# Weight-block sums on VectorE, finer waits of the partial copies and parts of 6, 6, 6 and 4 chunks in a two-layer decoder step

## The chip, the cores and the metric

The kernel runs on one core of a Trainium2 chip. The metric is device microseconds of one execution; three runs of the kernel before were timed, and one execution was profiled.

## What is computed

One step of a two-layer decoder trunk for 576 tokens (512 prompt tokens and 64 sample tokens, both with the same weights), width 1024, all in float32. Each layer is a feed-forward block (FFN), a mixer with three branches, and a second FFN. The change is in the two FFNs of each layer, four in all.

```
def swiglu(x, w_in, w_out):
    gate, up = jnp.split(x @ w_in, 2, axis=-1)          # w_in: 1024 x 5632
    return (jax.nn.silu(gate) * up) @ w_out             # w_out: 2816 x 1024

def hybrid_layer(x, p, ...):
    x = x + 0.5 * swiglu(rms_norm(x, p['ffn1_norm']), p['ffn1_w_in'], p['ffn1_w_out'])
    ...                                                  # mixer: attention, RG-LRU, short convolution
    x = x + 0.5 * swiglu(rms_norm(x, p['ffn2_norm']), p['ffn2_w_in'], p['ffn2_w_out'])
```

## The kernel before

Tokens lie along the free axis, so that a matmul has 128 weight columns and moves 288 tokens (half of 576). Float32 accuracy comes from a split: every operand is a rounded part and a rest (weights `whi` and `wlo`, inputs `hh`/`hl`, `bh`/`bl`, `ah`/`al`), and each product is three matmuls. ScalarE makes `whi` from the loaded weights `wraw`, VectorE makes `wlo` by subtraction.

The 2816 hidden columns of an FFN are taken in 11 steps of 256. The work is a list of units, written out in `ffn_units`:

- **up** s: the plain product for step s, four items (each 24 matmuls);
- **gate** s: the same size, but by a scheme with seven block products instead of eight (items 0 to 6, 12 matmuls each). It needs sums and differences of the four weight blocks (`wsum`, the weights of items 1 to 4), and of the moving blocks;
- **out** v: a part of the hidden steps times `w_out`, for 256 output columns, also by seven products; four units (v = 0 to 3) for each part;
- **last** v: the last part of the hidden steps, plain, without sums.

`PART_STEPS` says which hidden steps make a part: before these are 2, 3, 3 and 3 steps (a step is two chunks of 128, so 4, 6, 6 and 6 chunks), and the last is plain.

All engines walk the same list of items in order, each with its own queue. TensorE works on item i, ScalarE and VectorE split the item that takes i's place in a ring of four weight slots (`BEHIND[i]`, mostly item i+4). A unit's loads go into one of two `wraw` halves by DMAs that the SP queue issues in order.

Between the products of a gate unit ScalarE copies partial sums out of PSUM (`parts`, after items 0, 1, 2 and 4) into `kept`, `tmp5` and `tmp2`; item 2 must not start before the copy after item 0, item 3 not before the copy after item 1. Those buffers hold step s-1's hidden values until VectorE has made their split blocks, in four pieces (`moving_lo`, nth 1 to 4); `buffers_free` makes ScalarE wait for that. Step s-1's hidden values are computed on VectorE by `even_hidden` (behind item 6 of the gate) and `odd_hidden` (behind item 0 of the next up).

The weight sums are made by GpSimd (POOL) in `weight_sums`. `past_forgets` looks up 16 cache pages on SP, and the mixer's VectorE code waits for their DMAs. At the end of the second FFN VectorE also prepares sums of the next layer's inputs (`norm_sums`), and in the prologue it works out `decay` from a parameter.

Of the kernel before, what the change touches and what calls it, by code (L numbers as in the profile page):

```python
# [130 lines left out]
def ffn_items():  # L131
# [3 lines left out]
    for n, (kind, s, v) in enumerate(FFN_UNITS):  # L135
        if kind == "up" and s in (3, 6, 9):
            at += 1
# [60 lines left out]
def build(nc, t_in, t_out):  # L198
    S, plan = make_plan()
    with ExitStack() as ctx:  # L200
# [44 lines left out]
        with ExitStack() as m:  # L245
# [220 lines left out]
        def _(sp):  # L466
# [49 lines left out]
            def past_forgets(L):  # L516

                st, k = S["ffn1"], 2 * len(FFN_UNITS) - 1
# [8 lines left out]
            with sp.Fori(0, DEPTH) as L:  # L527
# [9 lines left out]
                past_forgets(L)  # L537
# [53 lines left out]
        def _(pe):  # L591
# [73 lines left out]
            def ffn(name, nn, L):  # L665
                st, f = S[name], nn // 2
                i = 0
                for n, (kind, s, v) in enumerate(FFN_UNITS):
# [6 lines left out]
                    for j in range(2):  # L675
                        slot = st.slot(2 * n + j)
                        for h in range(2):
# [7 lines left out]
                            for kk in range(half):  # L685
# [3 lines left out]
                                if kind == "last" and v == 0 and j == 0:  # L689
                                    pe.wait_ge(a_ready, L * 12 + (6 * f + c + 1))  # L690
# [281 lines left out]
        def _(act):  # L972
# [65 lines left out]
            def buffers_free(st, f, n, L):  # L1038

                kind, s, v = FFN_UNITS[n]  # L1040
                if kind == "out" and v == 0:
                    act.wait_ge(mov_ready, blocks_ready(L, f, PART_STEPS[s][-1], 4))
                elif kind == "gate" and FFN_UNITS[n - 1][0] == "out":
                    act.wait_ge(freed[st.slot(2 * n - 2)], st.turn(2 * n - 2, L) + 1)
                elif kind == "gate" and 0 < s <= 8:
                    act.wait_ge(mov_ready, blocks_ready(L, f, s - 1, 4))
                elif kind == "gate" and s > 8:
                    act.wait_ge(a_ready, L * 12 + (6 * f + 2 * (s - 8)))

            def parts(st, f, n, m, L):  # L1050
# [8 lines left out]
                if m == 0:  # L1059
                    buffers_free(st, f, n, L)  # L1060
# [3 lines left out]
            def ffn(name, nn, L):  # L1064
# [3 lines left out]
                for n, (kind, s, v) in enumerate(FFN_UNITS):  # L1068
                    for m in range(7 if n in SEVEN_NO else 4):
# [8 lines left out]
                        elif kind == "gate" and m == 6:  # L1078
                            if s < 8:
                                moving_first(f, s, s - PART_STEPS[(s + 1) // 3][0], L)  # L1080
                            act.wait_ge(gate_in, L * 44 + (22 * f + 2 * s + 2))
                            act.activation(tmp[5][:, 0:N], tmp[5][:, 0:N], ACT.Silu).then_inc(silu_ready, 1)
                        elif kind == "up" and m == 0 and 0 < s <= 8:
                            moving_second(f, s - 1, s - 1 - PART_STEPS[s // 3][0], L)
                        elif kind == "last" and m % 2:
# [6 lines left out]
                            else:  # L1092
                                norm_next(L, c, 24, L + 1, 0)
                                if c % 2:
                                    norm_sums(L * 16 + 16, c // 2)
# [220 lines left out]
        def _(dve):  # L1316
# [69 lines left out]

            def ring_split(st, f, i, L):
# [658 lines left out]
```

## Time and profile before

| | |
|---|---|
| median of 3 runs | 3035.36 us (3030.13 to 3038.66) |
| profiled execution | 3030.68 us, its span 3028.6 us |
| TensorE busy, of the span | 93% |
| VectorE busy | 72% |
| ScalarE busy | 44% |
| GpSimd busy | 19% |
| mean granted TensorE clock | 0.977 of full |

Busy shares are means over stages; the four FFNs lie at about 26 to 490, 1050 to 1525, 1525 to 1975 and 2560 to 3005 us of the span, the mixers between them.

### The profile page before, as it was taken

The numbers are of one execution on the slowest core, as the hardware profiler recorded it, in microseconds if no ns is written. First come the engines' busy times: TensorE is split into PE (matmuls) and PEld (weight loads), VectorE is DVE, ScalarE is ACT, GpSimd is POOL, SyncE is SP. The second block draws the span as 40 slices with busy tenths as digits, with TensorE's granted clock in tenths as the row PEclk, the third lists the DMA queues.
The fourth block names the chain that finished last, engine by engine and source line by source line (L and its number), as shares of the span: only waits on it lengthen the run. The fifth ranks groups of instructions, "written<-read, shape, count | busy, mean of one in ns | idle before, by whom it ended". The sixth has DMA issues, their size and how long they took to land.

```text
span 3028.6 us, 59749 instructions
## 1 busy us (share of the span) xinstructions
PE 2827.6 (93%) x20752; PEld 2742.9 (91%) x20752; DVE 2168.4 (72%) x3317; ACT 1331.2 (44%) x2393; POOL 579.7 (19%) x472
## 2 busy tenths in 40 slices
PE   4989999999999998989988989999999999989997
PEld 4888999898999998989988989999889999989897
DVE  5878776766655588778778778767766447878777
ACT  4444444455532344434444444435555223444444
POOL 2323321000000123323123323210000002323231
PEclk8999999999999999999999999999999999999999
DMA  2222222333222222222212222233332223122222
GB/s 87 84 77 77 73 89 79 103 95 88 83 83 83 85 77 78 76 79 84 85 64 77 77 78 84 85 91 87 88 94 80 83 83 98 57 84 85 74 91 77
DMA packets 299402, 250.31 MB, mean 83 GB/s; under 512 B 20899, under 2 KB 296563, under 8 KB 299175
## 3 DMA queue, kind: packets, MB, share of 16 engines
q1 hardware_dynamic: 297031, 242.44, 26.2%
q0 software_dynamic: 2144, 4.98, 0.5%
q8 instruction: 125, 2.05, 0.3%
q14 instruction: 102, 0.84, 0.1%
HBM read 240.04 MB, written 7.34 MB: 82 GB/s over the span
## 4 chain that ended last, share of the span: by engine, by line
PE 60%; DVE 17%; DVEq 8%; issue 7%; ACT 5%; SPq 1%; POOLq 1%; ACTq 0%; DMA 0%
PE ps L608 30%; PE ps L656 16%; PE ps L693 9%; DVE wlo L1394 5%; ACT whi L1021 2%; DVEq L1499 2%; DVE x L1498 2%; DVEq L1503 1%; DVE kept L1417 1%; DVE bl L1404 1%; DVEq L1432 1%; DVEq L1415 1%; DVE kept L1420 1%; PE ps L821 1%; DVE tmp L1445 1%
## 5 line engine op out<-in xcount | busy, mean ns | idle before, releaser
L1394 DVE TENSOR_TENSOR wlo<-wraw,whi 128x512 fp32r<-128x512 f32 (+2 forms) x500 | 382.1, 766 | 224.5 <-ACT whi L1021 218.6
L1325 DVE TENSOR_TENSOR wlo<-wraw,whi 128x1024 fp32r<-128x1024 f32 (+1 forms) x188 | 221.2, 1177 | 317.9 <-ACT whi L985 317.1
L1939 POOL TENSOR_TENSOR wsum<-wraw 128x512 f32<-128x512 f32 (+2 forms) x184 | 229.8, 1249 | 1049.6 <-DVE wlo L1394 683.3
L985 ACT ACTIVATE whi<-wraw 128x1024 fp32r<-128x1024 f32 (+1 forms) x188 | 191.6, 1020 | 393.6 <-PE ps L608 379.3
L608 PE MATMUL ps<-hh,whi 128*128 128x288 f32 x1664 | 362.1, 299 | 0.0
L608 PE MATMUL ps<-hl,whi 128*128 128x288 f32 x1664 | 357.7, 297 | 0.0
L608 PE MATMUL ps<-hh,wlo 128*128 128x288 f32 x1664 | 357.5, 296 | 0.0
L1021 ACT ACTIVATE whi<-wraw 128x512 fp32r<-128x512 f32 (+2 forms) x500 | 283.5, 571 | 119.8 <-PE ps L656 75.2
L1394 DVE TENSOR_TENSOR wlo<-wsum,whi 128x512 fp32r<-128x512 f32 (+2 forms) x368 | 270.5, 746 | 62.1 <-ACT whi L1021 61.3
L693 PE MATMUL ps<-hh,whi 128*128 128x288 f32 x1408 | 304.2, 298 | 8.9 <-DVE hl L1588 4.7
L693 PE MATMUL ps<-hl,whi 128*128 128x288 f32 x1408 | 303.7, 298 | 0.0
L656 PE MATMUL ps<-bh,whi 128*128 128x288 f32 x896 | 271.1, 303 | 34.8 <-DVE wlo L1394 21.5
L693 PE MATMUL ps<-hh,wlo 128*128 128x288 f32 x1408 | 302.8, 297 | 0.0
L656 PE MATMUL ps<-th,whi 128*128 128x288 f32 x704 | 220.3, 313 | 80.1 <-ACT kept L1062 80.1
L608 PEld LDWEIGHTS ps<-hh,whi 128*128 128x128 f32 x1664 | 269.1, 190 | 0.9
L608 PEld LDWEIGHTS ps<-hl,whi 128*128 128x128 f32 x1664 | 269.3, 190 | 0.0
L608 PEld LDWEIGHTS ps<-hh,wlo 128*128 128x128 f32 x1664 | 269.3, 190 | 0.0
L656 PE MATMUL ps<-bh,wlo 128*128 128x288 f32 x896 | 265.2, 296 | 0.0
L656 PE MATMUL ps<-bl,whi 128*128 128x288 f32 x896 | 264.8, 296 | 0.0
L1021 ACT ACTIVATE whi<-wsum 128x512 fp32r<-128x512 f32 (+2 forms) x368 | 198.2, 552 | 137.2 <-PE ps L693 86.3
L693 PEld LDWEIGHTS ps<-hh,whi 128*128 128x128 f32 x1408 | 228.9, 190 | 9.8 <-DVE hl L1588 5.0
L693 PEld LDWEIGHTS ps<-hh,wlo 128*128 128x128 f32 x1408 | 229.0, 190 | 0.0
(363 smaller groups left out, 6757.3 us busy)
## 6 DMA issues: line engine op xcount, KB each, us to landing
wraw<-in_ffn_w_in SPq DMA_DIRECT2D x88, 1024.0 KB
wraw<-in_ffn_w_out SPq DMA_DIRECT2D x48, 768.0 KB
wraw<-in_w_in SPq DMA_DIRECT2D x28, 1024.0 KB
wraw<-in_w_in SPq DMA_DIRECT2D x56, 512.0 KB
wraw<-in_w_branch SPq DMA_DIRECT2D x24, 512.0 KB
wraw<-in_w_out SPq DMA_DIRECT2D x9, 1024.0 KB
wraw<-in_ffn_w_out SPq DMA_DIRECT2D x16, 512.0 KB
kv<-in_cache_k SPq DMA_DIRECT2D x128, 64.0 KB, 1.9
```

Source lines behind the costliest of these rows:

```text
L608: last = pe.matmul(ps[slot][:, half, 0:HF], weights, rhs[:, k, half * HF:(half + 1) * HF], start=(start and c == 0 and n == 0), stop=(stop ...
L656: last = pe.matmul(bank, weights[:, kk, :], moving, start=(m in (0, 1, 5) and kk == 0 and t == 0), stop=(m in (3, 5, 6) and kk == half - 1 ...
L693: last = pe.matmul(ps[slot][:, e, 0:HF], weights[:, kk, :], moving[:, c, e * HF:(e + 1) * HF], start=(c == 0 and t == 0), stop=(c == 2 * h ...
L821: pe.matmul(logits(e, qb), qp[hs, qs], kp[hs, 0:n], start=True, stop=False, skip_group_check=True)
L985: act.activation(split_tile(into, j, rowwise), raw_tile(slot, j, rowwise), ACT.Copy).then_inc(hi_ready, 1)
L1021: ins = act.activation(ring(whi, i), weights_of(st, i), ACT.Copy)
L1325: dve.tensor_tensor(split_tile(lo, j, rowwise), raw_tile(slot, j, rowwise), split_tile(hi, j, rowwise).bitcast(F32), ALU.subtract).then_in ...
L1394: ins = dve.tensor_tensor(ring(wlo, i), weights_of(st, i), ring(whi, i).bitcast(F32), ALU.subtract)
L1404: dve.tensor_tensor(bl[:, a:b, kk, :], raw, bh[:, a:b, kk, :].bitcast(F32), ALU.subtract).then_inc(mov_ready, 1)
L1498: dve.tensor_tensor(down[:, HF:N], down[:, HF:N], other[:, 0:HF], ALU.add)
L1499: dve.drain()
L1939: pool.tensor_tensor(out, x0, x1, op).then_inc(wsum_ready, 1)
```

## The change

Its parts: (1) hidden steps go into parts of 3, 3, 3 and 2 steps, so the out units come after up 3, 6 and 9 and the plain last part has four chunks; (2) the four weight sums of every gate and out unit move from GpSimd to VectorE, each placed behind a ring split, two items ahead; (3) ScalarE waits for piece 1 before the copy after item 0 and for piece 3 before the copy after item 1, where before it waited for piece 4 ahead of the first; VectorE makes pieces 2 and 3 both behind item 1 of the up unit, and piece 4 behind item 2; (4) the page lookups move from behind the mixer's first loads to between the loads of up 10 and gate 10 of the first FFN; (5) `decays` moves from the prologue to behind gate 4 of the first FFN (of both layers); (6) the next layer's `norm_sums` come two or four tiles later.

```diff
-PART_STEPS = ((0, 1), (2, 3, 4), (5, 6, 7), (8, 9, 10))
+PART_STEPS = ((0, 1, 2), (3, 4, 5), (6, 7, 8), (9, 10))
+LAST = 9
+SUMS_BEHIND = {3: (0,), 5: (1,), 7: (2, 3)}
...
-        if s in (2, 5, 8):
-            units += [("out", s // 3, v) for v in range(4)]
+        if s in (3, 6, 9):
+            units += [("out", s // 3 - 1, v) for v in range(4)]
...
                     if kind == "up":
                         load(S[name], n, L, 0, (w1, 0, KD, s * 256 + FFN, 256))
+                        if name == "ffn1" and s == STEPS - 1:
+                            past_forgets(L)
...
-                st, k = S["ffn1"], 2 * len(FFN_UNITS) - 1
+                st, k = S["ffn1"], 2 * FFN_UNITS.index(("out", 2, 3))
                 wait_apart(sp, filled[st.slot(k)], st.turn(k, L) + 1)
...
-            def buffers_free(st, f, n, L):
+            def buffers_free(st, f, n, m, L):
                 kind, s, v = FFN_UNITS[n]
-                if kind == "out" and v == 0:
+                if kind == "out" and v == 0 and m == 0:
                     act.wait_ge(mov_ready, blocks_ready(L, f, PART_STEPS[s][-1], 4))
-                elif kind == "gate" and FFN_UNITS[n - 1][0] == "out":
+                elif kind == "gate" and m == 1 and FFN_UNITS[n - 1][0] == "out":
                     act.wait_ge(freed[st.slot(2 * n - 2)], st.turn(2 * n - 2, L) + 1)
-                elif kind == "gate" and 0 < s <= 8:
-                    act.wait_ge(mov_ready, blocks_ready(L, f, s - 1, 4))
+                elif kind == "gate" and m < 2 and 0 < s <= LAST:
+                    act.wait_ge(mov_ready, blocks_ready(L, f, s - 1, (1, 3)[m]))
...
+            def weight_sum(st, f, i, L, first=None):
+                n, m, _ = ITEMS[i]
+                if n not in SEVEN_NO or m not in SUM_AT:
+                    return
+                base = st.first_unit + n
+                a11, a12, a21, a22 = (block_of(st, n, kh, mh_) for mh_ in range(2) for kh in range(2))
+                x0, x1, op = ((a21, a22, ALU.add), (summed(n, 1), a11, ALU.subtract), (a12, summed(n, 2), ALU.subtract), (a11, a21, ALU.subtract))[m - 1]
+                dve.drain()
+                if first is not None:
+                    wait_done(dve, st, f, first, L)
+                if m == 1:
+                    dve.wait_ge(unit_loaded[base % 2], L * (plan["layer_units"] // 2 * 32) + (base // 2 + 1) * 32)
+                dve.tensor_tensor(summed(n, m), x0, x1, op).then_inc(wsum_ready, 1)
...
                 elif m == 1:
                     moving_lo(f, s - 1, 2, M_T2, M_T3 + 1, two(tmp[2][:, 0:N]), L)
+                    moving_lo(f, s - 1, 3, M_B21, M_B22 + 1, two(tmp[5][:, 0:N]), L)
                 elif m == 2:
-                    moving_lo(f, s - 1, 3, M_B21, M_B22 + 1, two(tmp[5][:, 0:N]), L)
-                else:
                     moving_lo(f, s - 1, 4, M_T4, M_T4 + 1, tmp[3][:, 0:HF].rearrange("p (a n) -> p a n", a=1), L)
...
                         for j in BEHIND[i]:
+                            if j == 4:
+                                weight_sum(st, f, j + 1, L, first=i)
                             ring_split(st, f, j, L)
+                            if j + 2 < len(ITEMS):
+                                weight_sum(st, f, j + 2, L)
...
                             even_hidden(f, s, L)
+                            if f == 0 and s == 4:
+                                dve.drain()
+                                decays()
...
                                 norm_next(L, c, 24, L + 1, 0)
-                                norm_sums(L, L * 16 + 16, c, L + 1, 0)
+                                for kk in SUMS_BEHIND.get(c, ()):
+                                    norm_sums(L, L * 16 + 16, 2 * kk, L + 1, 0)
+                                    norm_sums(L, L * 16 + 16, 2 * kk + 1, L + 1, 0)
...
             with pool.Fori(0, DEPTH) as L:
-                weight_sums(S["ffn1"], 0, L)
```

On VectorE the order changes behind item 6 of a gate unit and item 0 of the next up unit. Before (L1394 is a ring split, L1417 and L1420 are `even_hidden`, L1428 begins `odd_hidden`):

```order
L1394 TENSOR_TENSOR wlo<-wraw,whi 128x512
L1416 ISA
L1417 TENSOR_TENSOR kept<-kept,tmp 128x576
L1420 TENSOR_TENSOR kept<-kept 128x288
L1393 REGISTER_ALU
L1394 TENSOR_TENSOR wlo<-wraw,whi 128x512
L1427 REGISTER_ALU
L1428 TENSOR_TENSOR tmp<-tmp 128x576
```

And now (L1411 is the ring split, L1402 the sum, L1434 and L1437 are `even_hidden`, L1445 begins `odd_hidden`):

```order
L1411 TENSOR_TENSOR wlo<-wraw,whi 128x512
L1401 REGISTER_ALU
L1402 TENSOR_TENSOR wsum<-wraw 128x512
L1433 ISA
L1434 TENSOR_TENSOR kept<-kept,tmp 128x576
L1437 TENSOR_TENSOR kept<-kept 128x288
L1410 REGISTER_ALU
L1411 TENSOR_TENSOR wlo<-wraw,whi 128x512
L1402 TENSOR_TENSOR wsum<-wsum,wraw 128x512
L1444 REGISTER_ALU
L1445 TENSOR_TENSOR tmp<-tmp 128x576
```

One sum stands ahead of `even_hidden` (its register row belongs to the wait for the unit's load), one ahead of `odd_hidden`. Further on, behind items 1 to 3 of the up unit, VectorE had these rows before (L1404 are pieces 2, 3 and 4, L1445 reads the second up tile):

```order
L1394 TENSOR_TENSOR wlo<-wsum,whi 128x512
L1403 REGISTER_ALU
L1404 TENSOR_TENSOR bl<-tmp,bh 128x2x288
L1393 REGISTER_ALU
L1394 TENSOR_TENSOR wlo<-wsum,whi 128x512
L1403 REGISTER_ALU
L1404 TENSOR_TENSOR bl<-tmp,bh 128x2x288
L1445 TENSOR_TENSOR tmp<-tmp,ps 128x576
L1393 REGISTER_ALU
L1394 TENSOR_TENSOR wlo<-wsum,whi 128x512
L1403 REGISTER_ALU
L1404 TENSOR_TENSOR bl<-tmp,bh 128x288
```

Now the same stretch reads (L1421 are the pieces, L1462 the second up tile):

```order
L1411 TENSOR_TENSOR wlo<-wsum,whi 128x512
L1402 TENSOR_TENSOR wsum<-wraw,wsum 128x512
L1420 REGISTER_ALU
L1421 TENSOR_TENSOR bl<-tmp,bh 128x2x288
L1420 REGISTER_ALU
L1421 TENSOR_TENSOR bl<-tmp,bh 128x2x288
L1410 REGISTER_ALU
L1411 TENSOR_TENSOR wlo<-wsum,whi 128x512
L1402 TENSOR_TENSOR wsum<-wraw 128x512
L1420 REGISTER_ALU
L1421 TENSOR_TENSOR bl<-tmp,bh 128x288
L1462 TENSOR_TENSOR tmp<-tmp,ps 128x576
```

All pieces stand ahead of the second up tile, and two sums have come in between. On SP, before, the lookups stand behind the mixer's first two loads (L525 is the first of 16 lookup DMAs):

```order
L503 DMA wraw<-in_w_in 128x8x256
L347 ISA
L523 TENSOR_LOAD pages
L523 ISA x2
L525 ISA
L525 DMA lfp<-in_cache_logf 128x8
```

Now they stand behind the load of up 10, and gate 10's load (the L505 row at the end) behind the last of them:

```order
L505 DMA wraw<-in_ffn_w_in 128x8x256
L349 ISA
L527 TENSOR_LOAD pages
...
L529 DMA lfp<-in_cache_logf 128x8
L499 ISA
L505 ISA
L505 DMA wraw<-in_ffn_w_in 128x8x256
```

The L349 row is the wait for the end of the last out unit; what follows on SP, gate 10's load first, queues behind it and the 16 lookups.

## Rows read from the trace of the kernel before

**Rows 1.** The page: busy us, share of the span, instructions.

```profile
PE 2827.6 (93%) x20752; PEld 2742.9 (91%) x20752; DVE 2168.4 (72%) x3317; ACT 1331.2 (44%) x2393; POOL 579.7 (19%) x472
```

**Rows 2.** The waits of TensorE: total us, times, longest us.

```profile
PE ps L656 <- ACT kept L1062: 80.1, 32, 3.2
PE ps L656 <- DVE wlo L1394: 47.1, 40, 20.5
PE ps L656 <- ACT tmp L1062: 13.2, 13, 1.6
...
PE ps L693 <- DVE al L1411: 8.3, 8, 1.1
...
PE ps L781 <- DVE lf L1649: 7.4, 2, 3.7
...
PE ps L693 <- DVE wlo L1325: 4.2, 1, 4.2
```

**Rows 3.** Timeline of TensorE, then ScalarE, at one gate unit.

```profile
1210.80 0.61 PE L656 MATMUL ps<-th,whi 128*128 128x288 f32 x1 [2.94 <-ACT kept L1062]
...
1210.34 0.41 ACT L1062 ACTIVATE kept<-ps 128x288 f32<-128x288 f32 x1 [4.38 <-DVE bl L1404]
```

**Rows 4.** Timeline of VectorE behind the up unit ahead of it: start, us.

```profile
1200.50 0.69 DVE L1394 TENSOR_TENSOR wlo<-wraw,whi 128x512 fp32r<-128x512 f32 x1 [1.85 <-ACT whi L1021]
1201.11 0.75 DVE L1428 TENSOR_TENSOR tmp<-tmp 128x576 f32<-128x576 f32 x1
1201.93 0.46 DVE L1433 TENSOR_TENSOR tmp<-tmp,kept 128x288 f32<-128x288 f32 x1
1202.31 0.45 DVE L1434 TENSOR_TENSOR tmp<-tmp,kept 128x288 f32<-128x288 f32 x1
...
1203.23 0.75 DVE L1404 TENSOR_TENSOR bl<-kept,bh 128x576 fp32r<-128x576 f32 x1
1203.90 0.75 DVE L1445 TENSOR_TENSOR tmp<-tmp,ps 128x576 f32<-128x576 f32 x1
...
1209.86 0.45 DVE L1404 TENSOR_TENSOR bl<-tmp,bh 128x288 fp32r<-128x288 f32 x1
```

**Rows 5.** Timeline of VectorE, then GpSimd, behind that gate unit.

```profile
1223.38 1.60 DVE L1417 TENSOR_TENSOR kept<-kept,tmp 128x576 f32<-128x576 f32 x1 [0.16 <-issue]
1225.06 1.39 DVE L1420 TENSOR_TENSOR kept<-kept 128x288 f32<-128x288 f32 x1
...
1222.58 1.79 POOL L1939 TENSOR_TENSOR wsum<-wsum,wraw 128x512 f32<-128x512 f32 x1 [0.28 <-issue]
```

**Rows 6.** VectorE by line and shape: count, busy us, mean ns.

```profile
L1417 DVE TENSOR_TENSOR kept<-kept,tmp 128x576 f32<-128x576 f32 x44 | 59.2, 1346 | 7.3 <-issue 6.6 <-ACT tmp L1082 0.7
L1498 DVE TENSOR_TENSOR x<-x,tmp 128x288 f32<-128x288 f32 x48 | 56.9, 1185 | 0.0
```

**Rows 7.** Windows: us, busy PE, PEld, DVE, ACT, POOL, granted clock, DMA.

```profile
900.00:950.00 50.00, 50.00 (x377) 50.00 (x376) 22.53 (x26) 13.82 (x15) 0.00 (x0) 1.00 0.26 83
...
1212.00:1214.00 2.00, 2.00 (x11) 2.00 (x11) 0.69 (x1) 0.11 (x2) 0.00 (x0) 0.58 0.00 0
1220.00:1222.00 2.00, 2.00 (x17) 2.00 (x16) 1.91 (x5) 1.21 (x2) 0.99 (x1) 1.00 0.04 11
```

**Rows 8.** Timeline of TensorE at two out units, one after the other.

```profile
1281.35 0.40 PE L656 MATMUL ps<-bh,whi 128*128 128x288 f32 x1 [0.34 <-DVE wlo L1394]
...
1290.33 0.39 PE L656 MATMUL ps<-bh,whi 128*128 128x288 f32 x1 [0.34 <-DVE wlo L1394]
```

**Rows 9.** Timeline of SP: issue of a gate unit's load.

```profile
1215.73 0.39 SPq L503 DMA_DIRECT2D wraw<-in_ffn_w_in  x1
```

**Rows 10.** Timeline of SP, then VectorE, at the page lookups.

```profile
493.55 18.13 SPq L525 DMA_DIRECT2D lfp<-in_cache_logf  x16
...
512.90 0.23 DVE L1633 COPY lfp<-lfp 128x128 f32<-128x128 f32 x1 [7.14 <-DMA lfp<-in_cache_logf]
```

**Rows 11.** Timeline of VectorE in the prologue: the longest run of the decay's small operations.

```profile
58.66 1.62 DVE L1556 SCALAR_TENSOR_TENSOR spt<-spt 128x8 f32<-128x8 f32 x7
```

More of the change, by code:

```diff
@@ L135, in ffn_items @@
     for n, (kind, s, v) in enumerate(FFN_UNITS):
-        if kind == "up" and s in (3, 6, 9):
+        if kind == "up" and s in (2, 5, 8):
             at += 1
@@ L1421, in even_hidden @@
                 else:
-                    kept_whole(2 * (s - 8), kept[:, 0:2, :])
+                    kept_whole(2 * (s - LAST), kept[:, 0:2, :])
             def odd_hidden(f, s, L):
@@ L1428, in odd_hidden @@
                 dve.tensor_tensor(pf[:, 0:N], pf[:, 0:N], tmp[1][:, 0:N], ALU.mult)
-                if s >= 8:
-                    kept_whole(2 * (s - 8) + 1, two(pf[:, 0:N]))
+                if s >= LAST:
+                    kept_whole(2 * (s - LAST) + 1, two(pf[:, 0:N]))
                     return
@@ L1537, in ffn @@
                                 norm_next(L, c, 24, L + 1, 0)
-                                norm_sums(L, L * 16 + 16, c, L + 1, 0)
+                                for kk in SUMS_BEHIND.get(c, ()):
+                                    norm_sums(L, L * 16 + 16, 2 * kk, L + 1, 0)
+                                    norm_sums(L, L * 16 + 16, 2 * kk + 1, L + 1, 0)
                         i += 1
@@ L1561, in log1p, with decays @@
                 dve.drain()
+            def decays():
+                dve.wait_ge(consts_ready, 2)
+                log1p(spt[1][:], spt[2][:], spt[3][:], spt[4][:], spt[2][:])
+                dve.tensor_scalar(spt[3][:], lam, -1.0, 0.0, ALU.mult, ALU.max)
+                dve.drain()
+                dve.tensor_tensor(spt[4][:], spt[3][:], spt[2][:], ALU.add)
+                dve.drain()
+                dve.tensor_scalar(decay[:, :, 0, :], spt[4][:], -8.0, None, ALU.mult)
+                dve.tensor_scalar(decay[:, :, 1, :], spt[4][:], 8.0, None, ALU.mult)
             dve.memset(eps[:, 0:1], EPS)
@@ L1600, in _ @@
             dve.scalar_tensor_tensor(out=spt[0][:], in0=lam, scalar=-1.0, in1=lam, op0=ALU.mult, op1=ALU.max).then_inc(pre_done, 1)
-            dve.wait_ge(consts_ready, 2)
-            log1p(spt[1][:], spt[2][:], spt[3][:], spt[4][:], spt[2][:])
-            dve.tensor_scalar(spt[3][:], lam, -1.0, 0.0, ALU.mult, ALU.max)
-            dve.drain()
-            dve.tensor_tensor(spt[4][:], spt[3][:], spt[2][:], ALU.add)
-            dve.drain()
-            dve.tensor_scalar(decay[:, :, 0, :], spt[4][:], -8.0, None, ALU.mult)
-            dve.tensor_scalar(decay[:, :, 1, :], spt[4][:], 8.0, None, ALU.mult)
             with dve.Fori(0, DEPTH) as L:
@@ L1920, in add_squares @@
                         pool.tensor_tensor(tmp[6][:, 0:N], tmp[6][:, 0:N], tmp[2 + m % 2][:, 0:N], ALU.add).then_inc(sq_added, 1)
-            def weight_sums(st, f, L):
-                wait_apart(pool, filled[st.slot(0)], st.turn(0, L) + 1)
-                item = {(n, m): i for i, (n, m, _) in enumerate(ITEMS)}
-                last = None
-                for n in SEVEN_NO:
-                    base = st.first_unit + n
-                    a11, a12, a21, a22 = (block_of(st, n, kh, mh_) for mh_ in range(2) for kh in range(2))
-                    s1, s2, s4, s3 = (summed(n, m) for m in (1, 2, 3, 4))
-                    wait_apart(pool, unit_loaded[base % 2], L * (plan["layer_units"] // 2 * 32) + (base // 2 + 1) * 32)
-                    for m, out, x0, x1, op in ((1, s1, a21, a22, ALU.add), (2, s2, s1, a11, ALU.subtract), (3, s4, a12, s2, ALU.subtract),
-                                               (4, s3, a11, a21, ALU.subtract)):
-                        if m == 4:
-                            wait_apart(pool, comb_lo, comb(L, f, item[n, 1]))
-                        elif last is not None:
-                            wait_apart(pool, comb_lo, comb(L, f, item[last, 4 if m == 1 else m]))
-                        pool.tensor_tensor(out, x0, x1, op).then_inc(wsum_ready, 1)
-                        pool.drain()
-                    last = n
             add_squares(0)
             with pool.Fori(0, DEPTH) as L:
-                weight_sums(S["ffn1"], 0, L)
                 add_squares(L * 24 + 8)
```

38 lines of the change are left out of this document (17 added, 21 removed).

## The prediction

> **What bounds the kernel now.** I read the page first, then who waits for whom, then one cycle in order of time. TensorE is busy 93% of the span [rows 1], so time can come only from its waits, from its clock, or from fewer matmuls. Its waits are two kinds: 32 waits of 2.5 us mean on a partial copy in the gate units (80.1 us), and smaller ones in the out units: 47.1 us on `wlo`, of which one of 20.5 belongs to the prologue and some 3 to the layer turn, so 23, and 13.2 us on copies [rows 2]. At one gate unit the chain is plain: TensorE stands 2.94 us for ScalarE's copy, ScalarE stood 4.38 us for the last split piece (`bl`) [rows 3], and VectorE made that piece at 1209.86, done at 1210.31, at the end of an unbroken row of work since 1200.50 [rows 4].
>
> Why is VectorE late? Its `even_hidden` took 1.60 and 1.39 us beside a GpSimd sum of 1.79 us [rows 5], where operations of the same widths take 0.75 and 0.45 [rows 4]. Over the trace L1417 has a mean of 1346 ns and L1498 one of 1185 [rows 6], against those 750 and 450: 44 x 0.6 + 48 x 0.73 = 61 us on two lines alone. The GpSimd sums hold VectorE at the places that TensorE later waits for.
>
> The waits cost more than themselves: in 1212 to 1214, behind the 2.94 us of standing, the granted clock is 0.58, near the lower of its levels (1.2 instead of 2.4 GHz), with 11 matmuls in 2 us [rows 7] instead of 15. Along the timeline 21 of the 32 gate waits are followed by such a stretch, each worth 1.3 to 2.8 us, 36 us together by my count.
>
> **Prices.** A fed TensorE runs 377 matmuls in 50 us: 0.133 us each [rows 7]. So an up unit is 96 x 0.133 = 12.8 us, a gate product 1.6, a whole step 24.0. On VectorE, from start to next start: 0.61 us for 512 columns, 0.67 for 576, 0.38 for 288; a drain adds 0.82 - 0.67 = 0.15 [rows 4]. By a line through these, 384 columns take 0.48. A sum has the shape of a split, so 0.61 + 0.15 = 0.76, or 0.63 in an out unit.
>
> **Gate units.** Per step four sums add 3.0 us to VectorE; against that the lengthening goes, which in this step is (1.60 - 0.75) + (1.39 - 0.45) = 1.8 on `even_hidden` and, where two more operations of the step stand beside sums, as much again. So VectorE's work a step stays about the same, and its order decides. Counting from the end of a gate unit: its last two operations, two splits and the first sum end at 3.1; `even_hidden` 1.4 (4.5); ScalarE's conversion, silu and split, for which VectorE stood 1.85 [rows 4] (6.4); split and sum 1.4 (7.8); `odd_hidden` 2.1 and piece 1 0.67 (10.6); up tile 0.67, a split with 0.3 of waiting, a sum (13.0); pieces 2 and 3 (14.4); split and sum (15.8); piece 4 (16.2); up tile and the split for product 3 (17.5). Before, piece 4 came at 18.4: 1210.31 less the start, which is 1210.80 - 2.94 - 3.2 - 12.8 = 1191.9 [rows 3, 4].
>
> TensorE ends the up unit at 12.8, product 0 at 14.4, product 1 at 16.0. The copy behind product 0 now needs only piece 1 (10.6), the one behind product 1 only piece 3 (14.4): neither is late. The next in line is the split for product 3, 17.5 against a start at 17.6, so no slack. I take 0.15 us for each of 36 gate units (nine per FFN now), 5 us: 80 - 5 = **75 us won**, and the **36 us** of clock with the waits. Bounds: 0 to 1.8 us a unit (half the relief not given), so 0 to 65 us of new waits, and the clock's gain down to half. Queued behind the first sum's wait for its load on VectorE is all of `even_hidden`; a load issued at 1215.73 [rows 9] has the DMA engines idle by 1220 to 1222 [rows 7], 4.5 us, while VectorE comes to that sum 7 us behind the issue. It is covered by 2.5 us.
>
> **Out units.** VectorE's work per unit of six chunks: 7 splits of 0.48, 4 sums of 0.63, five operations of 288 (1.9), one of 576 (0.67), two drains: 8.8 us, against 63 x 0.133 = 8.4 of matmuls. So VectorE is the bound here, by 0.4 us. Before, these units came 8.98 apart with a wait of 0.34 [rows 8] and a restart that costs some 0.25. All of before: 36 us of waits [rows 2] and some 50 restarts, 49 us. Now: 36 units x 0.4 and twelve first units whose copy behind product 0 still waits for piece 4 (some 0.8 + 0.25): 27. **22 us won**; bounds 0 (saturation takes it all) to 45.
>
> At this place the Trainium skill speaks against the change. By "Perfetto Trace Analysis", section "Optimizing Scalar/DVE Operations", one offloads work to Scalar or even GpSimd when VectorE is saturated, and this change loads it. By rule alone the sums' 255 us (176 x 0.76 + 192 x 0.63) would lie in the open in the out units, and nothing would be won there; the same section warns that GpSimd and VectorE share a read port, which is what rows 5 look like.
>
> **Matmuls.** One step goes from plain to seven products: 12 matmuls per FFN, 48 x 0.133 = **6 us won**.
>
> **Last part.** It now starts with two ready chunks (1.6 us) ahead of the two late ones, before with four (3.2 us), so the wait for `al` (8.3 us in all [rows 2]) grows by 1.6 in each FFN, with one low-clock stretch: **8 us lost**; bounds 0 to 14. TensorE's share of the last part shrinks by 12.8 us, VectorE's eight normalisation steps don't. The turn between layers already waits there (4.2 [rows 2]), so the saving, counted above as if it were free, is partly lost: by counting VectorE's work up to the next layer's gate 0 I get 7 us at the turn and 1 at the end, **8 us lost**; bounds 0 to 25.
>
> **Decay.** 18 small operations of 1.62/7 = 0.23 us [rows 11], 4.2 us. They stood in the prologue, where root and reciprocal hide most of the removal (and a sum comes in): 1 us won. Behind gate 4 they lie ahead of the next `odd_hidden`; 1.9 us is covered by VectorE's wait for ScalarE, 2.4 is not: 2 x 2.4. **4 us lost**; bounds 0 to 8.
>
> **Page lookups.** The 16 take 18.1 us on SP, and VectorE stood 7.14 us for them in the mixer [rows 10], with TensorE's 3.7 behind it (7.4 in both layers [rows 2]) and low clock after: gone now, **12 us won**. But gate 10's load queues behind them. It was issued some 6.5 us after the out units end, now 19.4 after, and lands 4.5 later, at 23.9. VectorE stands for it from 13.7 (first sum of gate 10). TensorE is covered until 24.0 by gate 9 and up 10; then it waits for sum, `even_hidden` and split, 3.7, for the next split 2.6, and runs at low clock: 8 us, **16 lost** in two layers; bounds 0 to 25.
>
> **Sum.** -75 - 36 - 22 - 6 + 8 + 8 + 4 - 12 + 16 = -115 us. Against the profiled execution's 3030.7 that is 2916; the median of the runs shown lies 4.7 us above that execution, so I predict **2920**.
>
> **Rivals.** (A) VectorE becomes the bound in the gate units too: the relief from GpSimd is smaller, or the sums ahead of `even_hidden` weigh more, and the wait for product 3's split takes the copy's place. For it: no slack there, and 72% busy [rows 1] grows. Against it: piece 4 comes 2 us earlier by the same count. At 1.2 us per gate unit, with half the clock's gain: 2920 + 38 + 18 = 2976. (B) Gate 10's load is not late enough to hold anything, and product 3 never waits: 2920 - 16 - 5 = 2899. (C) Slower: the first sum stands for its load in every step. The wait is in front of `even_hidden`, so each us of it delays TensorE by one once 2.5 us of cover are used. 115 us over 36 units is 3.2, so it decides from a landing of 7 + 3.2 = 10.2 us on, or 3040 at 11. Against it: 4.5 us in this trace. (D) The copies' finer waits give nothing because the late thing is all of VectorE's row: then 3020 to 3035; against it: piece 3 already came a split and a piece (1.6 us with its tile) ahead of piece 4, and the copy that needs it has one product (1.6 us) more time.
>
> **Chances.** Forecast, 2890 to 2945: 0.62. A: 0.22. B: 0.08. C: 0.03. D: 0.05. Eight in ten: 2885 to 2980. A change under 0.3% (9 us) can't be told from none. Faster 0.93 (forecast, A, B), same 0.03 and slower 0.04 from C and D.
>
> **What would show it.** No rows of `kept` in the waits of TensorE beyond a few us; L1434 near 0.75 us; the granted clock at 1.00 in the middle of the FFNs; out units 8.7 to 8.8 us apart; TensorE's wait at gate 10 of the first FFN, with VectorE standing for a DMA ahead of it; no wait for `lf`. The prediction is wrong if `wlo` waits of over 1 us stand in each gate unit, or if VectorE stands for loads in every step.

## The result and the profile after

The changed kernel takes 2951.6 us (median of 4 runs, 2950.33 to 2952.45), against 3035.6 for the kernel before beside it: a ratio of 0.9725, with a 95% interval of 0.9708 to 0.9742. That is 84 us less, where 115 were forecast. It lies above the forecast's band (2890 to 2945) and below rival A's 2976, inside the range named for eight in ten (2885 to 2980). The profiled execution's span is 2948.6 us, 80.0 less than before.

The page first, the row that answers to [rows 1]:

```profile
PE 2809.5 (95%) x20704; PEld 2714.1 (92%) x20704; DVE 2171.7 (74%) x3719; ACT 1341.7 (46%) x2409; POOL 113.8 (4%) x104
```

VectorE has 402 instructions more and yet only 3 us more busy time: what it took over from GpSimd, it got back in shorter operations. Who TensorE waits for, as in [rows 2] (total us, times, longest):

```profile
PE ps L659 <- DVE wlo L1411: 61.2, 83, 17.6
PE ps L696 <- DVE al L1428: 12.1, 8, 2.4
...
PE ps L696 <- DVE wlo L1411: 10.5, 4, 4.2
PE ps L970 <- ACT yout L1314: 6.9, 1, 6.9
...
PE ps L696 <- DVE wlo L1327: 5.3, 1, 5.3
PE ps L659 <- ACT tmp L1064: 5.0, 12, 0.4
```

The row for `kept`, 80.1 us before, is gone, and so is that for `lf`. The 61.2 us on `wlo` hold the prologue (17.6), the turn between the layers (7.8) and gate 10 of the first FFN (10 in both layers); of the rest none is over 1.4. VectorE's two lines of [rows 6], by shape, and windows (columns as in [rows 7]) over 250 us of FFN steps with their out units, behind the wait at gate 10, and behind one in the last part of a second FFN:

```profile
L1434 DVE TENSOR_TENSOR kept<-kept,tmp 128x576 f32<-128x576 f32 x44 | 33.4, 758 | 7.9 <-issue 7.9
...
L1514 DVE TENSOR_TENSOR x<-x,tmp 128x288 f32<-128x288 f32 x48 | 21.5, 448 | 0.0
```

```profile
1150.00:1400.00 250.00, 244.65 (x1789) 238.91 (x1790) 209.94 (x390) 121.42 (x253) 0.00 (x0) 1.00 0.27 87
...
426.00:430.00 4.00, 3.20 (x12) 2.90 (x12) 3.76 (x7) 0.63 (x1) 0.00 (x0) 0.57 0.00 0
...
1469.00:1474.00 5.00, 5.00 (x21) 5.00 (x22) 4.22 (x6) 2.11 (x5) 1.58 (x1) 0.50 0.01 2
```

Means of 1346 and 1185 ns became 758 and 448, and the granted clock is 1.00 through the steady FFN. In the FFNs it is at or near the lower level (0.50, that is 1.2 of 2.4 GHz) only behind longer standing: 4.2 us in both of these places, 2.4 us for `al` at the start of the last parts, and at the prologue and the turn.

**Where the time went.** For each kernel I cut TensorE's timeline at the first matmul of each kind of unit (the wait ahead of it counts with the unit) and added up the pieces, in us:

| kernel | up | gate | out | last | both mixers | median us |
|---|---|---|---|---|---|---|
| before | 580.9 | 644.5 | 406.5 | 167.9 | 1181.0 | 3035.6 |
| after | 581.1 | 563.7 | 438.4 | 141.9 | 1171.3 | 2951.6 |
| fine_pool | 581.9 | 586.3 | 427.8 | 141.0 | 1171.5 | 2963.0 |
| coarse_dve | 581.9 | 655.0 | 451.9 | 143.0 | 1171.9 | 3060.1 |
| coarse_pool | 581.0 | 678.3 | 442.0 | 142.8 | 1172.0 | 3075.6 |
| before_fine | 580.6 | 563.6 | 394.7 | 169.4 | 1181.8 | 2940.8 |
| lookups | 581.8 | 548.4 | 438.4 | 141.5 | 1171.5 | 2934.8 |
| decays_spread | 581.7 | 562.4 | 436.5 | 140.1 | 1171.5 | 2945.5 |
| out_pool | 582.3 | 569.6 | 427.2 | 141.7 | 1171.3 | 2946.8 |
| parts_before | 578.7 | 547.2 | 417.9 | 165.8 | 1170.1 | 2933.7 |
| sums_end | 576.4 | 576.1 | 438.5 | 130.1 | 1171.5 | 2951.6 |
| sums_top | 582.3 | 562.5 | 436.7 | 140.3 | 1171.4 | 2937.9 |
| three | 580.5 | 538.5 | 413.3 | 164.2 | 1169.2 | 2911.6 |
| four | 579.3 | 545.5 | 394.6 | 167.3 | 1169.1 | 2900.1 |

With the parts of before, matmuls alone take 358.1 us of out and 153.4 of last (2688 and 1152 at 0.1332); with the parts after, 402.8 and 102.3. The kernel before, timed anew beside each group of runs, had medians of 3032 to 3036 us.

### The profile page after: what moved, and what is told of

Its sections match the earlier page's. It is cut to its first block, busy times and chain, and to the rows that moved or that the text cites. A ratio compares the mean times of both kernels' runs of the same rounds, so it can differ in the third digit from the quotient of the medians.

```text
span 2948.6 us, 58981 instructions
## 1 busy us (share of the span) xinstructions
PE 2809.5 (95%) x20704; PEld 2714.1 (92%) x20704; DVE 2171.7 (74%) x3719; ACT 1341.7 (46%) x2409; POOL 113.8 (4%) x104
## 4 chain that ended last, share of the span: by engine, by line
PE 57%; DVE 16%; DVEq 9%; issue 9%; ACT 5%; SPq 1%; POOLq 1%; DMA 1%; ACTq 1%; POOL 0%
PE ps L611 31%; PE ps L659 15%; DVE wlo L1411 5%; DVEq L1397 4%; PE ps L696 4%; ACT whi L1024 2%; DVE wsum L1402 2%; DVEq L1449 1%; DVE bl L1421 1%; POOLq L1945 1%; DVE kept L1434 1%; DVEq L1515 1%; PE ps L824 1%; PE ps L762 1%; PE ps L763 1%
## 5 line engine op out<-in xcount | busy, mean ns | idle before, releaser
L1411 DVE TENSOR_TENSOR wlo<-wraw,whi 128x512 fp32r<-128x512 f32 (+2 forms) x500 | 322.3, 650 | 154.8 <-ACT whi L1024 148.0
L1024 ACT ACTIVATE whi<-wsum 128x384 fp32r<-128x384 f32 (+1 forms) x368 | 207.3, 573 | 255.2 <-DVE wsum L1402 198.8
L659 PE MATMUL ps<-bh,whi 128*128 128x288 f32 x1008 | 306.9, 305 | 16.7 <-DVE wlo L1411 11.6
L659 PE MATMUL ps<-bh,wlo 128*128 128x288 f32 x1008 | 298.6, 296 | 0.0
L659 PE MATMUL ps<-bl,whi 128*128 128x288 f32 x1008 | 298.1, 296 | 0.0
L611 PEld LDWEIGHTS ps<-hl,whi 128*128 128x128 f32 x1664 | 267.9, 189 | 0.0
L696 PEld LDWEIGHTS ps<-hl,whi 128*128 128x128 f32 x1408 | 228.0, 190 | 0.0
L1411 DVE TENSOR_TENSOR wlo<-wsum,whi 128x384 fp32r<-128x384 f32 (+1 forms) x368 | 219.2, 616 | 11.7 <-ACT whi L1024 11.7
L659 PEld LDWEIGHTS ps<-bh,whi 128*128 128x128 f32 x1008 | 189.9, 188 | 33.8 <-ACT tmp L1064 15.7
```

The source lines that it names most:

```text
L611: last = pe.matmul(ps[slot][:, half, 0:HF], weights, rhs[:, k, half * HF:(half + 1) * HF], start=(start and c == 0 and n == 0), stop=(stop ...
L659: last = pe.matmul(bank, weights[:, kk, :], moving, start=(m in (0, 1, 5) and kk == 0 and t == 0), stop=(m in (3, 5, 6) and kk == half - 1 ...
L696: last = pe.matmul(ps[slot][:, e, 0:HF], weights[:, kk, :], moving[:, c, e * HF:(e + 1) * HF], start=(c == 0 and t == 0), stop=(c == 2 * h ...
L1024: ins = act.activation(ring(whi, i), weights_of(st, i), ACT.Copy)
L1411: ins = dve.tensor_tensor(ring(wlo, i), weights_of(st, i), ring(whi, i).bitcast(F32), ALU.subtract)
```

## The experiments

**Waits or sums.** Four kernels with the parts, decays, lookups and normalisation sums of the changed one, crossed: finer or coarse copy waits, sums on VectorE or GpSimd. Finer waits go with the new places of pieces 3 and 4 throughout; no run has the one without the other. The changed kernel is the corner with finer waits and VectorE.

fine_pool puts all sums back on GpSimd:

```
-                                weight_sum(st, f, j + 2, L)
...
+                weight_sums(S["ffn1"], 0, L)
```

> The changed kernel with its weight sums back on GpSimd; finer copy waits, parts and moved pieces stay. Theory 1 (order decides: VectorE's work in a step is about the same with either engine, and the finer waits do most of the work): the copy waits stay small, below 0.5 us a gate unit, and the time is 2950 to 2980. Theory 2 (relief decides: GpSimd's sums lengthen VectorE's operations, and freeing it of them is what won): L1417-like operations are back at 1.3 us mean, waits of 1 us and more stand in most gate units, and the time is 3000 to 3030.

Measured: 2963.0 us (2961.35 to 2966.5), ratio 0.9767 [0.9741, 0.9794]. VectorE by shape, and TensorE's first row of waits:

```profile
L1421 DVE TENSOR_TENSOR bl<-tmp,bh 128x576 fp32r<-128x576 f32 x72 | 87.3, 1254 | 0.0
L1434 DVE TENSOR_TENSOR kept<-kept,tmp 128x576 f32<-128x576 f32 x44 | 61.5, 1397 | 7.3 <-issue 6.7 <-ACT tmp L1084 0.7
```

```profile
PE ps L659 <- DVE wlo L1411: 83.3, 73, 19.3
```

VectorE's operations are as long as before, 1397 ns, and pieces 2 and 3 are lengthened too (mean 1254, against 749 in the kernel before); yet the waits for `kept` are gone. Theory 1 holds.

coarse_dve keeps the sums on VectorE and undoes the finer waits (all of `buffers_free` acts ahead of the first copy again, and pieces 3 and 4 of VectorE go back behind items 2 and 3):

```
-                elif kind == "gate" and m < 2 and 0 < s <= LAST:
-                    act.wait_ge(mov_ready, blocks_ready(L, f, s - 1, (1, 3)[m]))
+                elif kind == "gate" and 0 < s <= LAST:
+                    act.wait_ge(mov_ready, blocks_ready(L, f, s - 1, 4))
```

> The changed kernel with the copy waits of before (all partial copies of a gate unit wait ahead of the first for piece 4, and pieces 3 and 4 stand where they stood); sums stay on VectorE. Theory 1 (order decides): piece 4 comes at 16.2 us by the count of the prediction and the first copy is wanted at 14.4, so 32 gate units wait about 2 us and the clock falls behind many of them: 3000 to 3030. Theory 2 (relief decides): piece 4 is in time, no copy wait over 0.5 us, 2950 to 2970.

Measured: 3060.1 us (3057.3 to 3060.82), ratio 1.0087 [1.0061, 1.0113]: 0.9% above the kernel before, 30 us over theory 1's range and 90 over theory 2's. TensorE's waits and VectorE's line:

```profile
PE ps L659 <- ACT kept L1066: 77.4, 36, 3.6
PE ps L659 <- DVE wlo L1413: 48.4, 64, 16.7
PE ps L659 <- ACT tmp L1066: 18.5, 12, 1.6
```

```profile
L1436 DVE TENSOR_TENSOR kept<-kept,tmp 128x576 f32<-128x576 f32 x44 | 33.4, 759 | 7.9 <-issue 7.9
```

`even_hidden` is at its short 759 ns, and the copies are waited for in 36 gate units, 2.15 us each, where theory 1 had 32 waits of about 2. Relief without the finer waits wins nothing. What neither theory had in its sum: the first out units of the parts wait for the later piece 4 as well (18.5 us on `tmp` in 12 waits, 5.0 in the changed kernel). The gate units lose 91 us in all (655.0 against 563.7), 14 of them beside the copies' 77.4.

coarse_pool undoes both.

> The changed kernel with both undone: sums on GpSimd and the coarse copy waits. What is left of the change is the parts of 6, 6, 6, 4 and the moved decays, lookups and normalisation sums. By both theories the copy waits are back (36 gate units of some 2.5 us with their clock), and the parts, the last part and gate 10 cost some 30 us: 3030 to 3070. If it were near 2950, the gain would come from the parts and moved pieces, and both theories would fall.

Measured: 3075.6 us (3070.77 to 3076.8), ratio 1.0138 [1.0112, 1.0165], 6 us above the range expected, with the copy waits back:

```profile
PE ps L659 <- ACT kept L1066: 87.4, 36, 3.2
```

So the finer waits, with the pieces' new places, are worth 109 us with sums on VectorE (3060.1 - 2951.6) and 113 with sums on GpSimd (3075.6 - 2963.0); the sums' move is worth 11 and 15. That is a net price: between fine_pool and the changed kernel the gate units win 22.6 us (586.3 to 563.7) and the out units lose 10.6 (427.8 to 438.4). The rest of the change, with neither, costs 43 (3075.6 less the 3032.4 of the kernel before beside it).

before_fine is the kernel before with the finer waits (the same lines of `buffers_free`, with the counts of its own parts) and, as in the change, piece 3 behind item 1 of the up unit and piece 4 behind item 2.

> The kernel before with the finer copy waits and the earlier piece 3 alone; sums on GpSimd, parts, decays, lookups and normalisation sums as before. Theory (the finer waits win nearly all, whatever engine makes the sums): the gate units fall from 644.5 us by 70 to 90, the out units and last parts stay, 2930 to 2960. Rival (the finer waits only pay once the parts or the moved pieces are there): less than 60 us won, 2975 to 3010.

Measured: 2940.8 us (2939.49 to 2941.16), ratio 0.9692 [0.9675, 0.9709]: 11 us better than the whole change. The gate units fall by 81 us, as the theory had it; the out units fall too, by 12 us (406.5 to 394.7), which it had not. Two rows of TensorE's waits, without one for `kept`, and the timeline of VectorE, then ScalarE, in one of its up units and the gate unit behind:

```profile
PE ps L656 <- DVE wlo L1393: 75.9, 70, 21.1
...
PE ps L656 <- ACT tmp L1061: 1.9, 4, 0.6
```

```profile
1194.05 1.60 DVE L1416 TENSOR_TENSOR kept<-kept,tmp 128x576 f32<-128x576 f32 x1 [0.16 <-issue]
1195.72 1.39 DVE L1419 TENSOR_TENSOR kept<-kept 128x288 f32<-128x288 f32 x1
...
1204.02 2.51 DVE L1403 TENSOR_TENSOR bl<-tmp,bh 128x576 fp32r<-128x576 f32 x2
1207.06 0.45 DVE L1403 TENSOR_TENSOR bl<-tmp,bh 128x288 fp32r<-128x288 f32 x1
...
1205.58 0.41 ACT L1061 ACTIVATE kept<-ps 128x288 f32<-128x288 f32 x1 [0.95 <-PE ps L656]
...
1207.18 0.41 ACT L1061 ACTIVATE tmp<-ps 128x288 f32<-128x288 f32 x1 [0.59 <-PE ps L656]
```

The 1.60 and 1.39 us of [rows 5] stand there unchanged, and pieces 2 and 3 take 2.51 us. But the two copies, at 1205.58 and 1207.18, now wait for TensorE and not for VectorE: the second comes after piece 3, and piece 4, made at 1207.06, would have held the first by 1.9 us under the old wait (1207.06 + 0.45 - 1205.58).

**Gate 10.** lookups issues the page lookups behind gate 10's load:

```
                         load(S[name], n, L, 0, (w1, 0, KD, s * 256 + FFN, 256))
-                        if name == "ffn1" and s == STEPS - 1:
-                            past_forgets(L)
                     elif kind == "gate":
                         load(S[name], n, L, 0, (w1, 0, KD, s * 256, 256), apart=(s == 0))
+                        if name == "ffn1" and s == STEPS - 1:
+                            past_forgets(L)
```

> The changed kernel with the 16 page lookups issued behind the load of gate 10 instead of ahead of it. Theory (the lookups hold gate 10's load): the waits of 4 us at gate 10 of the first FFN go, with their low clock; 14 us won, 2934 to 2941, and still no wait for lf in the mixer. Rival (the hold only moves to the next load, that of the last part): less than 5 us won, 2946 to 2953, with a wait on wlo in the last part of the first FFN.

Measured: 2934.8 us (2934.14 to 2935.76), ratio 0.9672 [0.9647, 0.9698], 17 us won. In the changed kernel, SP, then VectorE, then TensorE stood like this:

```profile
399.02 18.18 SPq L529 DMA_DIRECT2D lfp<-in_cache_logf  x16
417.49 0.45 SPq L505 DMA_DIRECT2D wraw<-in_ffn_w_in  x1
...
422.85 0.69 DVE L1402 TENSOR_TENSOR wsum<-wraw 128x512 f32<-128x512 f32 x1 [11.13 <-DMA wraw<-in_ffn_w_in]
...
426.49 0.61 PE L659 MATMUL ps<-hh,whi 128*128 128x288 f32 x1 [4.18 <-DVE wlo L1411]
...
430.64 0.40 PE L659 MATMUL ps<-th,whi 128*128 128x288 f32 x1 [0.96 <-DVE wlo L1411]
```

In lookups gate 10 takes 11.19 us, as long as its matmuls, against 18.27 and 18.04 in the changed kernel, and the mixers keep what they won.

**Decays.** decays_spread deals the 18 operations out by twos:

```
-                            if f == 0 and s == 4:
-                                dve.drain()
-                                decays()
+                            if f == 0 and s < 9:
+                                decays(slice(2 * s, 2 * s + 2))
```

> The changed kernel with the 18 decay operations spread by twos over nine gate steps of the first FFN, where VectorE stands for ScalarE, in place of all at one step. Theory (they cost only where they outrun that standing): the gate unit at 14.7 us falls to 12.0 in both layers, others grow by less than 0.1, 5 us won: 2945 to 2948. Rival (every small operation delays the pieces, since VectorE has no slack there): within 2 us of 2951.6.

Measured: 2945.5 us (2944.14 to 2946.97), ratio 0.9706 [0.9689, 0.9723]: 6 us won. Gate 5, where the delay shows, falls from 14.67 and 14.70 us to 12.01 and 12.04. The gate units' sum falls by only 1.3 in this trace, since gate 10 of the second layer took 21.0 us instead of 18.0; over the runs in which the lookups hold its load gate 10 takes 14.4 to 21.1, and what moves it was not tried.

**Out units.** out_pool returns the sums of the out units alone to GpSimd (`weight_sum` returns for them; GpSimd's loop passes over gate units).

> The changed kernel with the sums of the out units alone back on GpSimd; those of the gate units stay on VectorE. Theory (in out units VectorE's own work is the bound, 9.03 us a unit against 8.4 of matmuls, and four sums there cost more than GpSimd's lengthening): out units go from 438.4 us in all to about 428, gate units stay within 2 us, 2940 to 2944. Rival (the hold of out units is the copy behind product 0 and the alternation with ScalarE, not VectorE's work): out units stay at 435 to 440, 2949 to 2954.

Measured: 2946.8 us (2944.8 to 2947.53), ratio 0.971 [0.9694, 0.9727]. Out units 427.2 us as the theory had it, 11.2 won, but the gate units gave 5.9 back, where the theory allowed 2: 5 us won, between the two expectations.

**Parts.** parts_before keeps everything but the split of the steps: `PART_STEPS = ((0, 1), (2, 3, 4), (5, 6, 7), (8, 9, 10))`, `LAST = 8`.

> The changed kernel with the parts of before (4, 6, 6, 6 chunks), all else as changed. Theory (the smaller last part no longer covers VectorE's normalisation work): the last parts fall from 39.6 us over their matmuls to 15 to 20, against 6.4 us more of matmuls; 2932 to 2945. Rival (the last part's loss comes from where the sums of the next norm stand, not from its size): excess stays above 30, 2950 to 2962.

Measured: 2933.7 us (2932.82 to 2934.46), ratio 0.9669 [0.9653, 0.9685]: 18 us better, 6.4 us more of matmuls included. The last parts' time over their matmuls falls from 39.6 to 12.4 us; the out units' rises from 35.6 to 59.8, most of it in the parts of four chunks, 29 to 30 us where matmuls take 22.4, and 7.7 in those behind the decays. Gate 10 stands no more: SP issues the lookups at 384.16 us, 15 earlier than in the changed kernel, since the out units that they wait for come one step earlier. So the time came out as the theory said, but not for its reason alone. What the last parts won (27.2 us) is used up by what the out units lost (24.2) and by 6.4 of added matmuls, which those two numbers don't contain; the gate units' 16.5 us (563.7 to 547.2), 13.9 of them gate 10's, make most of the gain.

**Sums of the next norm.** In the changed kernel the sums for chunks 0 and 1 stand behind chunk 3 of the last part, those for 2 and 3 behind chunk 5, those for 4 to 7 behind chunk 7, so none is moved by more than three chunks. sums_end: `SUMS_BEHIND = {7: (0, 1, 2, 3)}`.

> The changed kernel with all normalisation sums for the next layer behind chunk 7, none behind chunks 3 and 5. Theory (the 4.2 us wait on wlo in the last part of the second FFN stands behind the sums that follow chunk 3 on VectorE): that wait goes with its low clock, 5 to 7 us less in each of the two, but the turn between the layers and the end grow by the two pairs that now come later, 6 to 9 us each: 2948 to 2958. Rival (the wait stands behind the splits or the chunk updates): last parts unchanged at 38 us, and all is lost at the turn and the end: 2962 to 2975.

Measured: 2951.6 us (2950.39 to 2953.46), ratio 0.9727 [0.971, 0.9744]. In the changed kernel the wait in the last part of the second FFN stood like this, VectorE first, TensorE last:

```profile
1462.89 1.68 DVE L1344 TENSOR_TENSOR tmp<-x 128x288 f32<-128x288 f32 x1
...
1467.08 1.43 DVE L1363 TENSOR_TENSOR tl<-tmp,th 128x576 fp32r<-128x576 f32 x2
1468.42 0.42 DVE L1411 TENSOR_TENSOR wlo<-wraw,whi 128x256 fp32r<-128x256 f32 x1
...
1468.90 0.85 PE L696 MATMUL ps<-ah,whi 128*128 128x288 f32 x2 [4.21 <-DVE wlo L1411]
```

The eight operations of `norm_sums` and their drains fill 1462.89 to 1468.4, ahead of the split that TensorE wants. With the sums at the end, these last parts take 32.33 and 32.77 us instead of 38.36 and 38.56, but the up unit at the turn and the gate behind it take 48.1 instead of 42.5, and the wait for `yout` grows from 6.9 to 14.9: nothing won in all, as the theory had it.

sums_top has the last two pairs of these sums at the top of the layer's loop (and ahead of the loop only the first two pairs); ScalarE's part of these sums moves likewise. VectorE's lines:

```
-SUMS_BEHIND = {3: (0,), 5: (1,), 7: (2, 3)}
+SUMS_BEHIND = {3: (0,), 5: (1,)}
             with dve.Fori(0, DEPTH) as L:
                 dve.drain()
+                for c in range(4, 8):
+                    norm_sums(L, L * 16, c, L, 0)
```

> The changed kernel with the last two pairs of normalisation sums taken from the end of the second FFN to the top of the next layer (the first layer's from ahead of the loop), so that behind the last layer they fall away; the order of the work on VectorE and ScalarE between the layers stays. Theory (the end is longer because ScalarE's output copies queue behind these sums): the wait of 6.9 us for the output copy goes, 4 to 6 us won, 2945 to 2948, turn unchanged. Rival (the end waits for the last update of x on VectorE): within 2 us of 2951.6.

Measured: 2937.9 us (2936.31 to 2939.93), ratio 0.9681 [0.9664, 0.9697], 14 us won and not 4 to 6. In the changed kernel, ScalarE, then TensorE, at the end:

```profile
2938.13 1.30 ACT L1004 ACTIVATE th<-tmp 128x576 fp32r<-128x576 f32 x2 [3.00 <-DVE tmp L1353]
...
2939.34 4.66 ACT L1314 ACTIVATE yout<-ps 128x1024 f32<-128x1024 f32 x5
...
2940.39 1.97 PE L970 MATMUL ps<-const,x 128*128 128x128 f32 x8 [6.87 <-ACT yout L1314]
```

With sums_top there is no wait for `yout`; from the last matmul of the FFNs to the end of the span it takes 19.4 us instead of 27.0. Gate 0 is shorter in both layers too, 26.4 and 18.6 us instead of 30.9 and 21.1, which I did not expect. In the first layer it takes 29.4 to 34.6 us in the kernels without this edit and 26.4 to 27.9 in the three with it, so part of it is the edit's; what in it does that was not tried.

**Together.** three is parts_before, sums_top and decays_spread in one.

> The changed kernel with the parts of before, the last two pairs of normalisation sums at the top of the layer, and the decays spread. By the single runs the three add: 2933.7 - 13.7 - 5 to 8 = 2911 to 2916. If they stand in each other's way (sums and decays both lie on VectorE, whose slack the parts give): 2920 to 2928.

Measured: 2911.6 us (2910.42 to 2911.84), ratio 0.9596 [0.9579, 0.9612]. They add: singly they won 18, 14 and 6 us, together 40. four adds out_pool to it.

> The kernel of the run three with the sums of the out units on GpSimd as well. Theory (out units are bound by VectorE's work, the part of four chunks most, 7 us over its matmuls): out units fall from about 410 to about 396, gate units grow by up to 6: 2900 to 2908. Rival (GpSimd's lengthening of VectorE in the gate units next to it takes it back): within 3 us of three.

Measured: 2900.1 us (2899.13 to 2900.47), ratio 0.9557 [0.9541, 0.9574]: 51 us better than the changed kernel. Out units 394.6 us, gate units 7 us longer than in three, about as the theory had it (about 396, and up to 6).

## Why the prediction was right in sign and short in size

Step by step, from the pieces of TensorE's time (sum -80, as the span):

| term | forecast | measured |
|---|---|---|
| gate units: copy waits and clock | -111 | -103 |
| out units | -22 | -12.8 |
| matmuls | -6 | -6.4 |
| last parts | +8 | +25.1 |
| turn between layers | +7 | +6.0 |
| end | +1 | +4.9 |
| decays at gate 5 | +4 in all | +5.3, the prologue -3.1 |
| lookups, mixers | -12 | -9.7 |
| gate 10 | +16 | +13.9 |

The gate row is the -80.8 of the gate units less gate 10's +13.9, the decays' +5.3, the turn's +5.3 and the prologue's -2.2. Of the 35 us that are missing, 17 are in the last parts, 9 in the out units and 8 in the gate units.

**Gate units: right, and for the reason of the count, not of the opening.** The working counted VectorE's row operation by operation and found that its work per step stays about the same and "its order decides". The four crossed kernels show it: 109 to 113 us for the waits with the moved pieces, 11 to 15 for the sums. Whether the pieces had to move was not tried; by an estimate from the kernel before, not everywhere. There piece 3 was done at 1208.68 (1207.93 + 0.75 in the row below), a copy of 0.41 us behind it at 1209.1, and product 2, begun when product 1 ended at 1207.9, would have ended at 1209.5.

```profile
1207.57 0.30 PE L656 MATMUL ps<-th,wlo 128*128 128x288 f32 x1
...
1207.93 0.75 DVE L1404 TENSOR_TENSOR bl<-tmp,bh 128x576 fp32r<-128x576 f32 x1
```

One thing the working had wrong, and it did no harm: not all of the 32 waits were for piece 4. In the 12 gate units that stand behind out units, `buffers_free` waits for the last out tile to be added to x, and 27 of the 80.1 us are theirs. VectorE, ScalarE and TensorE at one of them, before:

```profile
1300.79 0.46 DVE L1505 SCALAR_TENSOR_TENSOR x<-ps,x 128x288 f32<-128x288 f32 x1
...
1301.34 0.41 ACT L1062 ACTIVATE kept<-ps 128x288 f32<-128x288 f32 x1 [4.01 <-DVE x L1505]
...
1301.81 0.40 PE L656 MATMUL ps<-th,whi 128*128 128x288 f32 x1 [2.05 <-ACT kept L1062]
```

The change moves this wait, too, from the first copy to the second (`m == 1` in the diff), and it is gone as well; but the prediction counted these 27 us as won by the count for piece 4, and that they went is luck.

The opening of the prediction answered "Why is VectorE late?" with GpSimd, from [rows 5, 6]. Those rows were true, but they didn't decide the copies' waits: fine_pool and before_fine have the same 1.4 us operations and no wait for `kept`. Moving the sums takes the lengthening away and puts the sums' own work on VectorE; the runs price only the two together, 11 to 15 us.

**Last parts: the step that failed.** The forecast gave them 8 us, by the wait for `al` alone, and put the lack of cover for VectorE at the turn. The wait for `al` did grow (8.3 to 12.1 us, longest 1.1 to 2.4, with low clock behind): in the first FFNs the last part's time over its matmuls grew by 4.3 us each. In the second FFNs it grew by 8.3 each: there the sums that now stand behind chunk 3 hold a split, 4.2 us and the low clock behind. sums_end took 5.9 us of that away in each, and put as much on the turn and the end, so between chunk 3 and the turn that work costs the same wherever it stands; sums_top shows that further on, at the top of the next layer, it costs less. parts_before shows the lack of cover from the other side: with three steps in the last part, 27 us of excess go, the growth of the `al` wait among them (back to 8.2 us).

In all, the new parts came out about even: going back to the old ones takes 27.2 us off the last parts and adds 24.2 to the out units and 6.4 of matmuls. What they did cost is gate 10's hold.

**Out units: the size was off.** I counted 8.8 us of VectorE work a unit; the units come 8.94 us apart at the place shown, with VectorE's row unbroken, and 9.13 in the mean (438.4 / 48). Over their matmuls the first unit of a part loses 0.66 us, where I took 1.05, and each of the other three 0.77, where I took 0.4. TensorE at two of them, as in [rows 8]:

```profile
1160.76 0.39 PE L659 MATMUL ps<-bh,whi 128*128 128x288 f32 x1 [0.20 <-DVE wlo L1411]
...
1169.70 0.39 PE L659 MATMUL ps<-bh,whi 128*128 128x288 f32 x1 [0.20 <-DVE wlo L1411]
```

That is hardly better than the 8.98 of before. Some 11 of the 12.8 us came from the part of four chunks, which took 28.0 us for 22.4 of matmuls and is no out part any more (4 x 5.6 = 22 us of excess before; 3.0 in each of the four parts that took their place). Of the 255 us of sums that the prediction set against these units, 134 are the gate units' (176 x 0.76). Here the rule that the prediction weighed, that it may make sense to offload work from a saturated VectorE, even to GpSimd (the Trainium skill, "Perfetto Trace Analysis", section "Optimizing Scalar/DVE Operations"), agrees with the runs for the out units: 427 to 428 us with sums on GpSimd, 438 with sums on VectorE. In the gate units it does not: 586.3 against 563.7.

**The end.** I gave it 1 us, seeing only VectorE's order. The output copies queue on ScalarE behind the rounding of sums that no layer uses.

**Gate 10 and the decays** went nearly as forecast: the load issued at 417.49, VectorE at 422.85; TensorE's first wait was 4.18 us for 3.7, its second only 0.96 for 2.6. The decays cost 2.7 us a layer for 2.4. parts_before adds what I had not seen: gate 10's hold belongs to the parts as well, since the lookups wait for the third group of out units, which the new parts bring one step later.

Rival A (VectorE the bound in gate units, too) happened in part. Leaving out gates 0 and 10 and the decays' delay, the gate units take 0.2 to 0.9 us over their matmuls, 0.54 in the mean and 19 us in all; I took 0.15, and A 1.2. Rival B (no hold at gate 10) falls with its wait of 4.18 us. Rival C (VectorE's first sum stands for its load in each step) shows only at gate 10. Rival D, that finer waits give nothing, falls with before_fine: they won 95 us (3035.9 - 2940.8) with the moved pieces alone, and all the rest of the change together gave back 11.

## What to carry to other kernels

Before an engine is unloaded, look for waits that cover several buffers, and split them: ask which of the pieces the waiting instruction overwrites, and when each is ready. That an engine's operations are lengthened is no loss until someone waits at the end of its row; count the row to the place that is waited for, once with the lengthening and once without. And a stage shortened on TensorE is worth only what the other engines' fixed work in it leaves: before cutting matmuls from a stage, add up the other engines' rows in that stage.

## What the runs showed of the hardware

Beside a GpSimd operation on SBUF, VectorE's operations with two SBUF inputs took up to 1.85 us instead of 0.42 to 0.76. Not each of them: of the 82 of 576 columns that a GpSimd addition or subtraction overlapped in the kernel before, half stayed near 0.76. The narrow ones can take as long as the wide: in the last parts of the changed kernel 14 splits of 256 columns took 1.60 to 1.64 us beside a GpSimd addition of 576 columns, two that it met for a shorter time 0.61 and 0.81, and all others 0.41 to 0.43. This row of VectorE stands beside one of GpSimd at the end of the changed kernel:

```profile
2918.95 1.59 POOL L1947 TENSOR_TENSOR tmp<-tmp 128x576 f32<-128x576 f32 x1 [2.57 <-ACT tmp L998]
...
2919.17 1.68 DVE L1344 TENSOR_TENSOR tmp<-x 128x288 f32<-128x288 f32 x1
```

By the Trainium skill, "SBUF — State Buffer", section "Who interferes with whom", such pairs of operations exclude each other, which agrees with these rows. What I had not expected is how little moving the sums won in all: 11 to 15 us of time for 61 us of lengthening on two lines; 22.6 won in the gate units and 10.6 lost in the out units, where the sums now fill VectorE's row (fine_pool against the changed kernel). What the lengthening alone costs no run shows.
